# Column sums of the adaptive rows on TensorE one group later in the second layer's gates, the last unit's after two products of the output projection

## The reference, cut to what matters

```
mod_x = silu(c) @ w_ada[l] + b_ada[l]          # 6 parts of 1024 columns
sh1, sc1, g1, sh2, sc2, g2 = split(mod_x, 6)
p_x   = (layer_norm(x) * (1 + sc1) + sh1) @ w_in[l]
g_f, g_m, g_g = split(sigmoid(gate_logits + b_gate), 3)
mix_x = (g_f * y_f + g_m * y_m + g_g * y_g) @ w_o
x = layer_norm(alpha * x + g1 * mix_x)
x = layer_norm(alpha * x + g2 * mlp(layer_norm(x) * (1 + sc2) + sh2))
```

## Time and profile before

| | |
|---|---|
| median of 3 runs | 3505.48 us (3504.45 to 3506.19) |
| profiled execution, its own time | 3496.41 us |
| its span | 3494.6 us |
| PE busy | 3157.9 us, 90% |
| DVE busy | 2026.3 us, 58% |
| POOL busy | 920.5 us, 26% |
| ACT busy | 986.7 us, 28% |
| granted clock, mean | 0.95 |

### The profile page before, as it was taken

One profiled execution on the slowest core, in us unless ns is written; L12 is line 12 of the kernel. 1 busy time (PEld: TensorE's weight loads), 2 busy tenths in 40 slices (PEclk: granted clock), 3 DMA queues, 4 the chain that ended last, 5 costly groups with the idle time before them and its releaser, 6 DMA issues. The chain is left out here.

```text
span 3494.6 us, 37458 instructions
## 1 busy us (share of the span) xinstructions
PE 3157.9 (90%) x15004; PEld 2457.2 (70%) x15004; DVE 2026.3 (58%) x2992; ACT 986.7 (28%) x1725; POOL 920.5 (26%) x606
## 2 busy tenths in 40 slices
PE   6998988999999999979898998799988888978788
PEld 3976656777478888778565665488878766777576
DVE  4576763444655555573675455666665846657354
ACT  3135761000231111131465000322222135421352
POOL 1004764221200000010377443200000325431263
PEclk9999999999999999989899999899999889999799
DMA  6511004343221212132101555132212310122100
GB/s 199 159 45 28 15 23 135 107 109 94 73 78 67 73 49 72 49 103 92 28 10 44 159 144 184 48 113 97 97 52 88 106 48 1 38 72 100 48 1 25
DMA packets 206333, 268.22 MB, mean 77 GB/s; under 512 B 29281, under 2 KB 133681, under 8 KB 205649
## 3 DMA queue, kind: packets, MB, share of 16 engines
q1 hardware_dynamic: 204080, 265.83, 23.7%
q10 hardware_dynamic: 2080, 0.01, 0.0%
HBM read 255.17 MB, written 10.52 MB: 76 GB/s over the span
## 5 line engine op out<-in xcount | busy, mean ns | idle before, releaser
L744 POOL TENSOR_TENSOR ht_lo<-HT,ht_hi 128x1024 fp32r<-128x1024 f32 x28 | 68.2, 2435 | 1108.8 <-ACT ht_hi L726 733.6
L1863 PE MATMUL ps<-ht_hi,w_hi 128*128 128x512 f32 (+1 forms) x768 | 273.7, 356 | 14.1 <-issue 12.5
L1863 PE MATMUL ps<-ht_lo,w_hi 128*128 128x512 f32 (+1 forms) x768 | 273.0, 355 | 0.0
L1863 PE MATMUL ps<-ht_hi,w_lo 128*128 128x512 f32 (+1 forms) x768 | 272.9, 355 | 0.0
L1873 PE MATMUL ps<-w_hi,a_hi 128*128 128x512 f32 x640 | 252.2, 394 | 4.3 <-DVE a_lo L1980 4.3
L1873 PE MATMUL ps<-w_hi,a_lo 128*128 128x512 f32 x640 | 251.0, 392 | 0.0
L1873 PE MATMUL ps<-w_lo,a_hi 128*128 128x512 f32 x640 | 250.9, 392 | 0.0
L366 PE MATMUL ps<-w_lo,ht_hi 128*128 128x320 f32 (+2 forms) x800 | 244.7, 306 | 0.0
L366 PE MATMUL ps<-gate_ht_hi,gate_w_hi 128*128 128x512 f32 (+1 forms) x576 | 226.8, 394 | 16.7 <-POOL w_lo L397 16.7
L1487 POOL TENSOR_TENSOR p_lo<-ring,p_hi 128x512 fp32r<-128x512 f32 x156 | 200.0, 1292 | 116.0 <-DVE p_hi L1442 88.6
L366 PE MATMUL ps<-U,ring 128*128 128x512 f32 (+1 forms) x576 | 217.9, 521 | 0.0
(11 more groups left out here) (414 smaller groups left out, 8066.0 us busy)
## 6 DMA issues: line engine op xcount, KB each, us to landing
ring<-w_dram SPq DMA_DIRECT2D x30, 2048.0 KB, 8.3
U<-w_ada_dram SPq DMA_DIRECT2D x80, 512.0 KB, 3.7
ring<-w_in_dram SPq DMA_DIRECT2D x48, 512.0 KB, 6.6
ring<-w_in_dram SPq DMA_DIRECT2D x8, 1280.0 KB, 5.9
ring<-a_w_in_dram SPq DMA_DIRECT2D x8, 1280.0 KB, 6.6
ring<-w_ada_dram SPq DMA_DIRECT2D x4, 2048.0 KB, 10.9
hi_scratch<-ht_hi SPq DMA_DIRECT2D x2, 3072.0 KB, 10.7
gate_ht_hi<-hi_scratch SPq DMA_DIRECT2D x8, 768.0 KB, 4.5
```

Of the source, the lines that this page charges most:

```text
L744: pool.tensor_tensor(HT_LO[:, :, tokens], HT[:, :, tokens], HT_HI[:, :, tokens].bitcast(F32), ALU.subtract).then_inc(ht_ready.sem, 1)
L1863: last = pe.matmul(ps[:, g % 4, 0:c1 - c0], lhsT, rhs, start=(k + j == 0), stop=(k == KD - 1 and j == 2))
```

## The change

In the second layer's gates (G is 3) PE sums the unit of the slot before ahead of group 2 in place of group 1; where G is 6 it stays at group 1. In both layers the last unit's sum leaves the end of the gates and stands after the projection's first two products, and DVE's take of it stands after the residuals of these two. ACT's wait for all units moves from the front of `mix_norm` to its third tile, where it first reads the columns.

```diff
@@ gemm
-                                if macs and g == 1:
+                                if macs and g == (2 if G == 3 else 1):
                                     macs.pe(pe, i * 2 + s - 1)
@@ gated
             gemm(G, mms, evac, 3, (("gpsimd", "gpsimd"), 24 * P, GATE_W, 3), False, ready, loads, macs)
-            macs.pe(nc.tensor, KD - 1)
-            macs.take(nc.vector, KD - 1)
@@ mix_norm, tensor
                         if i == 2:
+                            macs.pe(pe, KD - 1)
                             macs.all_taken(pe)
@@ mix_norm, vector
                     residual(0, 0)
                     residual(1, 0)
+                    macs.take(dve, KD - 1)
                     norms(0, residual(0, 1))
@@ mix_norm, scalar
-                    macs.all_taken(act)
                     for t in range(nq):
+                        if t == 2:
+                            macs.all_taken(act)
```

## The result

The changed kernel takes 3484.05 us (median of 6 runs, 3480.65 to 3486.46), the kernel before 3505.84 us beside it (median of 6, 3495.26 to 3512.44). The ratio is 0.9934, with a 95% interval of 0.9918 to 0.9951: 23 us faster, between 17 and 29. Forecast were 18.2 us, 3487.3. The median 3484.05 lies 0.5 us inside the forecast range of 3483.5 to 3497.5; the ratio, carried to the level that the prediction used (3505.5), gives 3482.3, 1.2 us past its fast edge.

A forecast was written before the change was run, and what follows sets the result against it. PE, busy 90% of the span, was held in the second layer's gates by waits for DVE's L589 and falling clock. 13.8 + 2.5 - 0.75 + 2.7 = 18.2 us off 3505.5 gave 3487.3 us, range 3483.5 to 3497.5.

The forecast's parts named there:

- What bounds the gates: Second layer's gates: PE waits for DVE's L589 and the clock falls behind some waits; moving the sum gains 13.8 us.
- The second limit: Second layer's gates: the refill circle takes 55.9 us per two slots; PE waits about 0.7 us for `w_lo` at slot starts.
- Rival (a): Second layer's gates: the refill, at 13.2 us, nearly replaces the wait; 11 us gained in all, 3494.5 us; chance 0.22.
- all will be spaced: Second layer's gates: q2 and q3 will be 3.5 us apart in every refill, so the refill takes 11.5 us.
- (c): Gates: the refill limit and a clock still falling at new waits leave 6 us gained, 3499.5 us; chance 0.10.
- (d): Gates: half clock for a whole group behind each new wait makes the kernel 5.8 us slower, 3511 us; chance 0.04.
- POOL and DVE: Second layer's gates: DVE's last pieces lie under POOL's splits, so its last four L589 take 8 to 9 us.
- The end of the second layer: Second layer's projection: the third product starts 19 to 20 us after the gates; 2.5 us gained, bounds 1.5 and 3.5.
- The end of the first layer: First layer's projection: the third product starts later, since no wait stood there; 0.75 us lost, bounds 0.5 and 1.5.
- The table load: Both projections: ACT's function table load waits for nothing, DVE's root wait falls from 1.61 to 0.27 us; 2.7 us gained.
- The sum: Whole kernel: the gains and losses of all steps add up to 18.2 us.
- (b): Second layer's gates: no second limit, PE runs at 27.6 us a slot; 21.6 us gained in all, 3484 us; chance 0.12.

The follow-up runs named there:

- the loop alone: The kernel before with only the sum moved to group 2 in the second layer's gates; 3487.51 us, ratio 0.9952.
- both comparisons: The changed kernel timed twice, unchanged, against the kernel before: 3484.05 us, ratio 0.9934, then 3486.51 us, ratio 0.9953.
- The end's edits alone: The changed kernel with the gates' sum back at group 1, run twice against the kernel before: 3490.65 us, ratio 0.9964, and 3487.12 us, ratio 0.9956.

## Why the prediction came out as it did

- **What bounds the gates: right.** The waits for L589 went, and the gates took 12.4 and 12.8 us less in the two profiles of the changed kernel and 13.7 in that of the loop alone, where 13.8 were forecast. As the step had it, that is more than the waits: of the 12.4 us, 6.9 are idle time of PE (9.9 us before, 3.0 after) and 5.5 are busy time of the same 806 matmuls (229.64 to 224.14), at a clock of 0.99 in place of 0.97.
- **The second limit: right in kind, its refill mis-sized.** PE's wait for `w_lo` came at three of six slots and not at each, with 0.47 to 1.30 us. The circle was counted at 55.9 us for two slots, 28.0 each; where it held PE up it took 56.8 to 57.6, and the 28.3 is the average with slots that it did not hold. The mis-sized term is the refill: 11.5 us were forecast, and the six that feed these slots took 12.6, 13.0, 13.1, 11.4, 13.0 and 12.5, 12.6 on average. The prediction read two refills of the kernel before and took the lower; the trace has six there, of 13.6, 13.3, 11.4, 12.8, 13.3 and 13.2 us. Its reason has support: where SP issued its last two loads of w_ada 3.5 us apart, the refill took 11.4 before, and 11.4 and 12.5 after; where they were 1.6 us apart it took 12.6 to 13.6. What failed is "all will be spaced": two of six were. That the gain still came out within 1.8 us is in part luck, since DVE's last piece ended 20.9 us after group 1 in two of the three circles with a wait, against 21.5 counted. Rival (a), 29.2 us a slot and 6.6 us of gain, fell by the sum, though its refill of 13.2 was nearer in five cases of six. (c) and (d) fell with the clock, which was 1.00 behind each of the new waits.
- **POOL and DVE: right.** The forecast 8 to 9 us for the last four L589 came as 8.73 in the slot shown, and 6.78 in the slot before it, where POOL had begun 9.4 us ahead of them (2062.18) and not 6.6. By the rule of the Trainium skill on the port that the two share (page SBUF — State Buffer, section "Who interferes with whom") this is what a DVE instruction with two SBUF inputs pays; the trace agrees, with 3.17 us for four in the free and 8.73 under the splits.
- **The end of the second layer: right.** Third product at 19.1 us against 19.4; 4.1 us less in the first profile and 3.1 in the second, for 2.5 + 1.34 forecast. Two small misses cancel in the first profile: the first two products took 13.9 us, without the 1.0 of low clock left to them, and the third stood 2.8 us behind them and not 2.35. In the second profile the two took 15.6 us.
- **The end of the first layer: right.** Forecast was -0.75 + 1.34 = +0.6; 0.4 measured.
- **The table load: right.** 1.34 us in each layer were forecast, and alone it gave 1.4 in each.
- **The sum: 16.9 of 18.2 us in the touched stretches**, 16.3 in the second profile; both comparisons pooled give 18.8 us.
- **What failed is the last step, from the sum to the time.** "I carry the difference and not the level" took 3505.5 as the level, the median of three runs that lay within 1.7 us of each other, and did not ask what the 9 us to the profiled execution were. They lie within the spread of this program, which took 3491.5 to 3512.4 us with a standard deviation of 4.8; the median of three stood 2.4 us above the mean of 54. Then "the range goes from (b) to beyond (a)" gave the fast edge, 3483.5, the bound of the kernel's own terms and nothing for the comparison, though the same part said that a measurement tells only 7 us from no change. The first comparison, 23 us with an interval of 17 to 29, lies past the 22 us of that edge; the second, 16 us, inside it. The forecast of 18.2 is in the interval of both. An edge 5 to 7 us further on each side, 3477 to 3503, would have been what that 7 us asked for. That (b)'s 21.6 us is nearer to the first ratio is no sign for (b): its mark, 27.6 us a slot with no wait of PE, did not come.

**Open.** The end's edits alone ran 12.7 us under the kernel before in the mean of 13 executions, and their rows account for some 3. Two profiles don't show where the other 9 to 10 us are: the gates took 240.7 us in both, none less than before, and the stretch behind took 1239.0 in one and 1248.7 in the other. Both profiled executions were slower than the median of their kernel (3492.6 against 3490.7, 3498.6 against 3487.1), so the quick ones have no profile. For the other kernels the ratio stands between 3.5 us below the rows of the touched stretches and 6.2 above them; for the end alone it stands 9.5 and 12 above. Whether an earlier projection makes clock falls behind it rarer, or the executions drew well twice, these runs don't tell. It isn't additive either: loop alone 16.8 us and end alone 12.6 by their ratios make 29, more than the whole change gave in either comparison.

## What to carry to other kernels

A wait is best followed one step further back than its releaser: here DVE was late because a refill, queued on SP behind DVE's own last piece, set POOL's work on top of it, and issuing the refill first removed the waits that moving the sum only stepped around. When a wait is moved away, count the circle that comes next in full, since it gave this change its size to 0.3 us a slot; and read every instance of a term that varies, here six refills and not two. And read a level and its spread from executions of the same program before a range is set: sum what the touched stretches say, and then widen it by what the untouched ones do.

## What was not expected of the hardware

- The same instructions, 5454 matmuls in the stretch behind the projection, took from 1235.4 to 1248.7 us in the profiles of these kernels, and 1235.4 and 1247.9 in two of the changed kernel alone; in windows of 15 us at nearly the same place the granted clock was 1.00 in one execution of the kernel before and 0.64 in another. Nothing in the program differed.
- DVE's instructions under POOL's run are paced by POOL's and not slowed by a factor: L589 takes 0.77 to 0.79 us in the free, and under the splits one completed for each of POOL's, so that three under them and one behind took 8.73 us.
- With DVE's pieces off the splits, PE's gates took 223.1 to 223.3 us in three kernels, whether the sum stood before group 1 or group 2.
